# Prompt attention spread from 32 into 42 slots of a paged decode step, and what moves with it

## The reference, cut to what matters

```python
z = xn @ w_in                      # conv B | conv C | conv x | q | k | v | forget | gates
y_conv = (cb * short_conv(cc * cx)) @ w_up_conv
# prompt: 8 heads of 64, causal, with forget sums dcum = cumsum(log f)
p = softmax(q k^T / 8 + dcum[q] - dcum[k]);  out = p v
# new tokens: 4096 cached keys and values each, in pages of 128 found by a page table
sp = q k_past^T / 8 + d_new + rev;  p = softmax([sp, sn]);  out = p v_past + p_new v
mixed = sigmoid(gA) * y_conv + sigmoid(gB) * (attention @ w_up_attn)
```

## Time and profile before

| | us |
|---|---|
| median of 3 executions | 2220.89 |
| lowest, highest | 2208.26, 2222.94 |
| the profiled execution | 2212.26 |
| span from its first to its last instruction | 2210.5 |

### The profile page before, as it was taken

How to read it: one execution, slowest core, us unless ns; L and a number is a source line. 1 busy time by engine, 2 the same in 40 slices (tenths; PEclk the granted TensorE clock), 3 DMA queues, 4 the chain that set the end, 5 groups by cost and what they waited for, 6 DMA issues and landing times.

```text
span 2210.5 us, 34385 instructions
## 1 busy us (share of the span) xinstructions
PE 2033.8 (92%) x12878; PEld 1207.7 (55%) x12878; DVE 716.0 (32%) x1649; ACT 487.3 (22%) x1057; POOL 259.3 (12%) x402
## 2 busy tenths in 40 slices
PE   6999987999987999999999999899499999999994
PEld 4577765666653666788888446754333333333331
DVE  5222213666640131333333541533411111111115
ACT  3212212544430100111111112322122222222223
POOL 1001221222223000000000000000011111111110
PEclk9999998999997999999999999999799999999997
DMA  8345786888888111310110220303899999999976
GB/s 320 119 145 185 257 304 231 266 280 288 264 266 282 67 48 40 104 58 10 58 48 27 83 95 1 143 20 110 300 364 383 384 376 367 377 374 374 371 272 241
DMA packets 205070, 458.69 MB, mean 208 GB/s; under 512 B 18721, under 2 KB 44338, under 8 KB 204778
## 3 DMA queue, kind: packets, MB, share of 16 engines
q1 hardware_dynamic: 172330, 357.96, 46.0%
q0 software_dynamic: 32576, 98.53, 12.9%
HBM read 432.51 MB, written 32.17 MB: 210 GB/s over the span
## 4 chain that ended last, share of the span: by engine, by line
PE 81%; DMA 6%; DVE 4%; issue 3%; ACT 2%; SPq 2%; DVEq 1%; POOLq 0%; ACTq 0%; POOL 0%
PE ps L1558 10%; PE ps L1044 10%; PE ps L1305 9%; PE ps L1589 5%; PE ps L1312 5%; PE ps L1569 5%; PE ps L1071 5%; PE ps L1171 5%; PE ps L1342 4%; PE ps L1598 3%; PE ps L1086 2%; DMA kraw<-in_cache_k 2%; PE ps L1431 2%; PE ps L1207 2%; PE ps L1182 2%
## 5 line engine op out<-in xcount | busy, mean ns | idle before, releaser
L1044 PE MATMUL ps<-xnT,ring 128*128 128x352 f32 x768 | 231.7, 463 | 1.7 <-ACT xnT L719 1.7
L1558 PE MATMUL ps<-gu,xgT 128*64 128x512 f32 x1024 | 226.8, 595 | 0.9 <-ACT xgT L1908 0.9
L1044 PEld LDWEIGHTS ps<-xnT,ring 128*128 128x128 f32 x768 | 145.9, 191 | 88.8 <-issue 8.5
L2821 POOL DMA_DIRECT2D vpage<-in_cache_v x256 | 137.4, 537 | 432.7 <-issue 423.8
L1171 PE MATMUL ps<-consts,kraw 128*128 128x128 f32 x1024 | 142.1, 283 | 27.5 <-DMA kraw<-in_cache_k 17.5
L1171 PEld LDWEIGHTS ps<-consts,kraw 128*128 128x128 f32 x1024 | 115.4, 144 | 60.5 <-issue 30.9
L2172 DVE COPY kt<-ps 128x512 f32<-128x512 f32 x128 | 88.3, 691 | 182.9 <-PE ps L1171 182.3
L1558 PEld LDWEIGHTS ps<-gu,xgT 128*64 128x64 f32 x1024 | 70.7, 137 | 131.9 <-issue 128.8
L1589 PE MATMUL ps<-wd,hidT_a 128*64 128x512 f32 x512 | 118.6, 605 | 17.4 <-ACT hidT_a L1918 11.5
L2712 DVE TENSOR_TENSOR sig_a<-ps,sig_a 128x256 f32<-128x256 f32 x32 | 13.6, 424 | 323.0 <-ACT sig_a L1912 323.0
L1569 PE MATMUL ps<-gu,xgT 128*32 128x512 f32 x1024 | 115.8, 592 | 0.0
(11 more groups left out here) (428 smaller groups left out, 2874.1 us busy)
## 6 DMA issues: line engine op xcount, KB each, us to landing
kraw<-in_cache_k SPq DMA_DIRECT2D x256, 256.0 KB, 3.6
vpage<-in_cache_v POOLq DMA_DIRECT2D x256, 256.0 KB, 4.7
gu<-in_w_expert_gate SPq DMA_DIRECT2D x32, 2048.0 KB, 20.2
gu<-in_w_expert_up SPq DMA_DIRECT2D x32, 2048.0 KB, 24.9
wd<-in_w_expert_down SPq DMA_DIRECT2D x31, 2048.0 KB, 21.4
ring<-in_w_in SPq DMA_DIRECT2D x8, 1024.0 KB, 7.0
yy<-y_d SPq DMA_DIRECT2D x16, 512.0 KB, 10.9
early<-in_w_in SPq DMA_DIRECT2D x6, 1024.0 KB, 10.5
```

Source lines behind the costliest of these rows:

```text
L1044: last = nc.tensor.matmul(bank(R.bank(*tag))[:, 0:NC_], slot[:, k, f * P:(f + 1) * P], xnT[:, k, cols_of(n)], start=k == 0, stop=k == KD - 1)
L1558: last = nc.tensor.matmul(bank(0)[h * BA:(h + 1) * BA, :].rearrange("p (x n) -> p x n", x=2), src[:, k, 0:BA], weight[:, k, :, h * DE // 2 ...
L2821: pool.dma_start(vpage[n % VS][:, p, :], t["cache_v"][ds(page, 1)].rearrange("a s d -> (a s) d")).then_inc(v_in[n % VS], 16)
```

## The change

- The 32 prompt units are spread over slots 29 to 70 (`UNIT_AT`, k * 43 // 32 behind slot 29). Slots 32, 36, 40 and so on up to 68 have none, nor have 71 to 73.
- The loop runs over 74 slots. Slots 64 to 73 have no keys, only a value unit and, in slots 65, 66, 67, 69 and 70, a prompt unit. Value units 54 to 63 are all weighed there, and no longer in front of the "conv C" products.
- "conv C" weights go to half 1 of the ring, and are asked for when the scores of key unit 63 are made, before the last prompt unit. "conv x" goes to half 0, behind the input's return. The other weights swap halves; the cross attention's output weights `xo` and its query weights `xq` swap places on SP's queue.
- The forget rows: the first 128 columns of pair 0 are asked for first (2 x 64 KB), then the rest of pair 0; pair 1 is asked for at key unit 36 instead of together with pair 0; pairs 2 and 3 at 43 and 55 instead of 41 and 49. Unit 0 waits for the first pieces, unit 1 for the rest.
- On DVE the masked sum of the last sequence (`mask_own(7)`) moves from behind the last softmax steps to the loop's slot 73.

```diff
-RING_ORDER = ["cc", "cx", "cb", "xk", "xv", "g0", "g1", "g2", "g3", "mo0", "mo1", "xq", "xo"]
+RING = {"cc": 1, "cx": 0, "cb": 1, "xk": 0, "xv": 1, "g0": 0, "g1": 1, "g2": 0, "g3": 1, "mo0": 0, "mo1": 1, "xo": 0, "xq": 1}
...
-        PROMPT0, KOUT0 = 29, 30
+        PROMPT0, PROMPT_SLOTS, KOUT0 = 29, 43, 30
...
+        UNIT_AT = {PROMPT0 + k * PROMPT_SLOTS // NU: k for k in range(NU)}
+        END = max(UNIT_AT) + 1
...
-            return [(n - PROMPT0, 0), (n - PROMPT0, 1)] if PROMPT0 <= n < PROMPT0 + NU else []
+            return [(UNIT_AT[n], 0), (UNIT_AT[n], 1)] if n in UNIT_AT else []
...
-        LOADS = {"cc": (w3(t["w_in"], O_CC), None), "cx": (w3(t["w_in"], O_CX), ("sq", NSU - 1)),
+        LOADS = {"cc": (w3(t["w_in"], O_CC), ("sq", NSU - 1)), "cx": (w3(t["w_in"], O_CX), ("po", NU - 1)),
...
-                 "xq": (w3(t["w_xq"], 0), ("m6", 0)), "xo": (w3(t["w_xo"], 0, D), ("m3", PAIRS - 1))}
+                 "xo": (w3(t["w_xo"], 0, D), ("m6", 0)), "xq": (w3(t["w_xq"], 0), ("m3", PAIRS - 1))}
...
-                    load_negk(0), load_negk(1)
-                if n == 41:
+                    for p in range(2):
+                        sp.dma_start(negk[0][p][:, 0:P], neg_d[p:p + 1, 0:P].to_broadcast([P, P])).then_inc(nd_in, 16)
+                    load_negk(0)
+                if n == 36:
+                    load_negk(1)
+                if n == 43:
                     load_negk(2)
-                if n == 49:
+                if n == 55:
                     load_negk(3)
 
+            ring_load(sp, "cc")
             R.made(sp, "po", NU - 1)
             for n in range(COLS):
                 sp.dma_start(xnT[:, :, cols_of(n)], xn_d[:, :, cols_of(n)]).then_inc(xn_in[n], 16)
             sp.wait_ge(stage_stored[0], 16 * 5), sp.wait_ge(stage_stored[1], 16 * 4)
-            ring_load(sp, "cc"), ring_load(sp, "cx")
+            ring_load(sp, "cx")
...
-            for n in range(NSU):
-                sample_scores(n)
+            for n in range(NSU + LAG):
+                if n < NSU:
+                    sample_scores(n)
...
-            weigh_pages(NSU - LAG), weigh_pages(NSU - LAG + 1)
-            turn_sample_probs(DB - 1)
             pe.wait_ge(s_max, DB)
             R.pe_free(pe, "turn")
             nc.tensor.transpose(bank(5)[0:DB, 0:P], negmax, ident).then_inc(R.full, 1)
             for x, (f, n) in enumerate(FN):
-                if x < SU:
-                    weigh_pages((DB - 1) * SU + x)
                 pe.wait_ge(xn_in[n], 16)
                 product(("cc", f, n), "cc", f, n)
...
-                    if k % PT == 0:
+                    if k == 0:
+                        dve.wait_ge(nd_in, 48)
+                    elif k == 1 or k % PT == 0:
                         dve.wait_ge(negk_in[k // PT % 2][p], 16 * (k // PT // 2 + 1))
```

More of the change, by code:

```diff
@@ L493, in build_program @@
                 add_keys(n, c)
-        for n in range(NSU):
-            R.add("dve", "sq", n, banks=(5,))
+        for n in range(NSU + LAG):
+            if n < NSU:
+                R.add("dve", "sq", n, banks=(5,))
             if n + 2 < NSU:
@@ L523, in build_program @@
                 R.add("dve", "so", (n - LAG) // SU, banks=(6,))
-            if n > SU and n % SU == 1:
+            if SU < n < NSU + SU and n % SU == 1:
                 add_probs(n // SU - 1)
-        R.add("dve", "so", DB - 2, banks=(6,))
-        add_probs(DB - 1)
         R.add("dve", "turn", banks=(5,))
         for x, (f, n) in enumerate(FN):
-            if x == SU - 1:
-                R.add("dve", "so", DB - 1, banks=(6,))
             R.add("act", "cc", f, n, banks=(0, 1, 2, 3, 7))
@@ L789, in ring_load @@
                 R.made(sp, *after)
-            dst = ring[n % 2] if src.shape[1] == KD else ring_xo
+            dst = ring[n] if src.shape[1] == KD else ring_xo
             for x in range(ring_parts(name)):
                 if ring_parts(name) == 2:
-                    sp.dma_start(dst[:, :, x * 256:(x + 1) * 256], src[:, :, x]).then_inc(ring_in[n % 2], 16)
+                    sp.dma_start(dst[:, :, x * 256:(x + 1) * 256], src[:, :, x]).then_inc(ring_in[n], 16)
                 else:
-                    sp.dma_start(dst, src).then_inc(ring_in[n % 2], 16)
+                    sp.dma_start(dst, src).then_inc(ring_in[n], 16)
         def ring_slot(pe, name):
-            n = RING_ORDER.index(name)
-            pe.wait_ge(ring_in[n % 2], 16 * sum(ring_parts(x) for x in RING_ORDER[n % 2:n + 1:2]))
-            return ring[n % 2]
+            n, loaded = RING[name], 0
+            for other in RING:
+                loaded += ring_parts(other) if RING[other] == n else 0
+                if other == name:
+                    break
+            pe.wait_ge(ring_in[n], 16 * loaded)
+            return ring[n]
         def samples(row):
@@ L878, in load_negk @@
                         R.read(sp, "ps", k, len(chunks(k)) - 1, p)
-                    sp.dma_start(negk[hp % 2][p], neg_d[2 * hp + p:2 * hp + p + 1, 0:SEQ].to_broadcast([P, SEQ])
+                    c0 = 0 if hp else P
+                    sp.dma_start(negk[hp % 2][p][:, c0:SEQ], neg_d[2 * hp + p:2 * hp + p + 1, c0:SEQ].to_broadcast([P, SEQ - c0])
                                  ).then_inc(negk_in[hp % 2][p], 16)
@@ L2198, in _ @@
                 copy_keys(n, 1), copy_keys(n, 3)
-            for n in range(NSU):
-                join_scores(n)
+            for n in range(NSU + LAG):
+                if n < NSU:
+                    join_scores(n)
                 copy_keys(n + 2, 1)
@@ L2203, in _ @@
                     biased(0, 0)
-                if n == PROMPT0 + NU:
+                if n == END:
                     take_prompt(NU - 1)
@@ L2225, in _ @@
                     mask_own(n // SU - 2)
-            mask_own(DB - 2)
             R.made(dve, "turn")
```

26 lines of the change are left out of this document (10 added, 16 removed).

## The result

The kernel after takes 2238.89 us in the median of 4 executions (2236.82 to 2241.4); the kernel before, run beside it, 2221.09. The ratio is 1.0101, with a 95% interval from 1.0077 to 1.0124: about 1%, 18 to 22 us, slower. The forecast was 13 us faster. The profiled execution of after took 2236.82 us (span 2235.1; before: 2210.5), so the two profiled executions stand further apart, 24.6 us, than the medians do.

A forecast was written before the change was run, and what follows sets the result against it. TensorE was taken as the bound in slots 30 to 61, so idle time on both sides counted: 12.6 won at the end, 5 lost in the slots, 5 won at the start, say 13 off 2220.9, giving 2208; range 2194 to 2224.

The forecast's parts named there:

- The end: End of the slots to the products: prompt units cover the values, loss falls from 28 to 15.4 us, 12.6 won.
- (a): From slot 71, no prompt unit left: unit 63 lands late, first product at T + 16.5 instead of T + 6.1; loss 10.4.
- (b): Slots 62 to 70: TensorE waits for DVE and ACT, with a wait for value units 54 and 58; loss about 5.
- the 6.4: Time in us of a value unit on a queue shared with keys alone: four issues, then 4.7 to landing.
- The slots without a unit: Slots 32 to 60: eight short slots leave keys less time beside other loads; 5 us lost, bounds 1 and 20.
- The start: Start of the prompt units: forget rows in pieces remove DVE's second wait; 5 us won, 2 to 7.
- Costed at nothing: The late `xq` weights, "conv x" behind the input, the moved `mask_own(7)` and POOL's queue order were taken to cost 0.
- Keys become the bound: Rival: every slot loses 0.6 us to keys, 20 us; 2223, decided by key waits over 18 us; chance 0.09.
- The stall moves: Rival: at the end unit 63 and the input's return collide worse; nothing won, 2221; chance 0.14.
- the signs of being right: Value waits 8 to 12 us behind slot 70, none over 2 before; key waits 2 to 8; forget wait ended near 366.
- the signs of being wrong: An `xnT` wait before the first product; ACT or DVE waits over 10 us in slots 62 to 70; key waits over 15.
- The 382 GB/s: The most the DMA engines were taken to deliver, used to time loads such as 1 MB in 2.7 us.

The follow-up runs named there:

- e11: The changed kernel with prompt units in 32 slots, forget rows of pairs 2 and 3 at key units 41 and 49, last ten value units alone: 2247.77 us.
- e12: e11 with the last eight value units in front of products 0 to 7 again: 2213.32 us.
- e4: The changed kernel with value units 61 to 63 weighed in front of products 5 to 7 of conv C: 2233.68 us.
- e8: The changed kernel with early page numbers, four buffers for the last value units, 36 prompt slots, last eight value units in front of products 0 to 7: 2189.53 us.
- e5: The changed kernel with each unit's page numbers read before the wait for its buffer, on SP and POOL: 2204.89 us.
- e1: The kernel before with only the new forget rows (pair 0 in pieces, pair 1 at key unit 36): 2213.41 us.
- e3: The changed kernel with four buffers for the last eight value units, the two key buffers included: 2228.63 us.
- e10: The changed kernel with page numbers read early on SP alone (keys): 2211.12 us.
- e9: The changed kernel with page numbers read early on POOL alone (values): 2251.94 us.

## Why the prediction was wrong

The time is 31 us above the forecast and above the range, and the sign is the other one. (Between the profiled executions, from the scores of unit 29 to the last product, 12.6 won was forecast and 22.8 lost came out: 35 us.) By the steps of the prediction:

- **The end: 12.6 won, measured 6.6 lost. This step failed, and 19 of the 35 us are here.** The loss before was read rightly: 28, by the table 28.2. The loss after was put at (a) 10.4 and (b) 5, and is 34.8. What failed in the prediction's terms is the time of a value unit: "covered, as long as two slots last over 6.4 us" in (b), and the moments of issue in (a). Both leave out the 2.9 us in front of the first issue. What failed in its reasoning is that it counted the prompt units as new cover and left out that the same edit takes old cover away: the eight value units stood in front of 40 us of products, whose own work left 1.6 us of waits for all eight. In the changed kernel the products come behind all values, and cover nothing. e11 against e12 prices this at 34.5 us. The spread has to earn that back first. From e11 to after the end goes from 143.6 us to 149.6 less 32 of moved prompt work, so the spread pays 26 there; in the slots 30 to 60 it costs 250.6 plus 32 less 265.2, 17. From e12: 34.5 lost, 26 won, 17 lost, 26 in all slower (2213.3 to 2238.9). With nothing lost in the slots it would still have been 8.5 slower than e12, and so about as slow as the kernel before.
- **(a), behind slot 70: right in place, too small in size.** T, the end of value unit 60, is 696.36 in after. Unit 62 was issued at T + 2.9 and unit 63 at T + 8.4, not at T and T + 3.1, because the page numbers are read in between and unit 61 was itself late. Unit 63 then took 9.0 us, near the 9.05 to 10.55 assumed. The first product began at T + 21.3 instead of T + 16.5: a loss of 15.2 instead of 10.4, within its bound of 16. That the value waits, 12.2, come so near to the 8 to 12 forecast is in part luck. The working has one wait there, and there are three. Nor would the waits of these units, taken away, have given their time back: e4 shows a wait of 10 for the input behind them. The prediction had "the first part of the input is then there: it has had over 10 us", and for after that holds; it doesn't once the units are gone.
- **(b), slots 62 to 70: 5 forecast, some 17 measured.** From the scores of unit 61 to T there are 12.5 idle and about 5 by half clock. The 5 were nearly all to come from other engines, and the waits for DVE there were 0.9 us; the waits for values were 10.4, of units 54, 58 and 60, and none over 2 had been forecast. With unit 61 the four had 7.8, 5.3, 10.7 and 6.6 us between their free buffer and the moment TensorE was ready for them, and needed 13.7, 8.6, 11.8 and 8.8. Of that 2.9 lay in front of the first issue, for unit 60 6.0: POOL paused for 2.8 us between two issues of unit 59, as in the kernel before and without a cause that the profile shows. Behind it lay 5.7 to 5.9, for unit 54 10.8, beside the 2 MB of "conv C" asked for at 643.78. The mis-sized term is the 6.4: by it only unit 58 would have waited, and 1.1 us.
- **The slots without a unit: 5 lost, measured 19. Right in kind, failed in size.** Key waits rose by 6.0, to 7.0 us, near the 5 that I took. Two things weren't in the sum: value waits of 7.3, which I didn't cost at all, since the earlier trace rows had none, and 6.4 of half clock. The prediction saw for keys that a load beside them makes them late and left the values out; 6.0 of the 7.3 are the two units beside such loads, which with the 2.9 in front needed 15.0 and 13.1 us. The half clock stands behind these two waits alone; in e8, where TensorE was idle for 4.9 of 251.2 us, the clock is 1.00. Experiment e5 shows what part the reading has: with the page numbers read ahead, slots 30 to 60 are 15.8 us shorter and the clock loss is 1.7. The loads beside them weren't tested by themselves.
- **The start: 5 won, measured 3.8 (e1: about 4). Right, slightly large.** I had the first piece there at 365.6; it was used at 368.05, as late as the whole row before. What went is the second wait, and so most of the wait for ACT. The rule on small transfers (the Trainium skill, DMA: Bandwidth & Descriptors, Bandwidth) has 0.95 us for 64 KB; the estimate from it, 3 won, lies about as near to the 3.8 as my 5. No row confirms it: the first piece was issued at 359.62 and used at 368.05, 8.4 us later, and how much of that the keys in front of it took can't be told.
- **Costed at nothing: right, as far as tested.** e12 equals e1. The start of `xq`'s use is 22.8 us later than before, like all else behind the products.
- **The rivals.** "Keys become the bound" had the sign of the result, but its place was wrong: keys cost 7.6 up to slot 63, far from the 18 from which it decides. "The stall moves" came nearest in mechanism: it named the end, and gave 2221. None of the rivals had the loss of the products' cover or waits for values in the slots.
- **The signs.** Of the signs of being right one held (key waits of 2 to 8 us); value waits behind slot 70 were just over theirs, 12.2 for 8 to 12. Three failed: value waits over 2 us in slots 64 to 70, a first forget wait that ended at 368.05 instead of near 366, and a wait for ACT of 2.48. None of the signs of being wrong appeared, though the forecast was wrong: none of them looked at values in front of slot 71.
- **The 382 GB/s** that the prediction takes as the most is the mean of the kernel before from 650 to 690; the same trace has 388 from 365 to 375. No sum above hangs on the difference.

The ends side by side: before and e12 have about 20 us of value waits with the products as cover, e11 48 without any, after 22.6 with prompt units as cover. The new cover took the place of the old one and added nothing to it.

## What to carry to other kernels

When an edit puts work behind a stalled transfer as cover, write down both lists: what will stand beside the transfer, and what stands there now and will no longer. Here taking eight transfers out from between the products cost 34.5 us, and the new cover paid 26. And count a transfer from the moment its buffer is free to its landing, not from its issue: what the issuing engine reads between its wait and its first issue belongs in front of the wait, which here was worth 20 to 34 us for an edit of a few lines when both queues had it, and nothing when only the values' queue did.

## What the runs showed of the hardware

- Reading four page numbers on an issuing engine takes about 2.25 us, 0.56 for each, as long as the four issues themselves (2.29): in e3 POOL issued one unit per 4.55 us. Read ahead of the wait, the first issue follows the free buffer after 0.18 us for keys (e5, e10) and 0.68 for values (e5, e9).
- Two queues that share the DMA engines aren't independent in their timing. Issuing values 2.2 us earlier (e9) made a key unit land after 9.14 us instead of 6.86, with 35.5 us of waits for keys instead of 7.0 in the one execution profiled; doing the same to both queues made the kernel faster by 34 us.
- Short waits cost more than themselves: behind waits of 2.24 to 7.38 us in the rows of after and e11 a value unit took 1.75 to 1.94 instead of 1.06 us, and the granted clock was 0.50, which is 1.2 instead of 2.4 GHz (from 475.0 to 481.8, behind the wait that ended at 474.73). The one at 682.31, behind 3.31, took 1.12: there the clock fell behind it, to 0.50 from 683.2 to 686.6. Of the 22.8 us that after lost, about 9 are this.
